# Two float32 blocks on one core: the slots of the split-weight ring get different offsets within 64 bytes

## What is computed

```python
def squared_relu_mlp(hn, w_up, w_down):
    return jnp.square(jax.nn.relu(hn @ w_up)) @ w_down

def first_block(x, ...):
    h = x
    for i in range(DEPTH):                       # 2
        hn = rmsnorm(h, mix_norm_g[i])
        mix = gated_deltanet(...) if i % N_MIXERS == 0 else moba_layer(...)
        h = h + mix.astype(h.dtype)
        h = h + squared_relu_mlp(rmsnorm(h, mlp_norm_g[i]), mlp_w_up[i], mlp_w_down[i])
    return rmsnorm(h, final_norm_g)
```

## Time and profile before

| | |
|---|---|
| median of 3 runs | 1252.89 us (1252.87 to 1253.22) |
| span of the profiled execution, first to last instruction | 1249.1 us |
| the profiled execution's own time | not recorded apart; the median is 3.8 us over the span |
| instructions in the span | 21,521 |
| moved by DMA | 210.80 MB |

### The profile page before, as it was taken

One profiled execution on the slowest core, in us unless ns is written; L12 is line 12 of the kernel. 1 busy time (PEld: TensorE's weight loads), 2 busy tenths in 40 slices (PEclk: granted clock), 3 DMA queues, 4 the chain that ended last, 5 costly groups with the idle time before them and its releaser, 6 DMA issues.

```text
span 1249.1 us, 21521 instructions
## 1 busy us (share of the span) xinstructions
PE 1220.7 (98%) x8583; PEld 1106.9 (89%) x8583; DVE 871.6 (70%) x1252; ACT 700.5 (56%) x1016; POOL 56.3 (5%) x102
## 2 busy tenths in 40 slices
PE   8999989999999999999999999999999999999997
PEld 7999988888888998888888999999999977888886
DVE  5888567666666656666656589998656577778876
ACT  4984555555455554554554564656454456666663
POOL 5010020000000001000000000000000010000000
PEclk9999999999999999999999999999999999999999
DMA  7671134666554654565555565354546534555561
GB/s 223 197 203 68 38 122 150 222 214 202 186 184 151 203 165 141 166 211 180 184 185 167 172 210 184 118 162 145 179 150 203 186 107 147 174 194 190 201 201 68
DMA packets 160340, 210.80 MB, mean 169 GB/s; under 512 B 5542, under 2 KB 143220, under 8 KB 160261
## 3 DMA queue, kind: packets, MB, share of 16 engines
q1 hardware_dynamic: 157315, 202.77, 50.6%
q0 software_dynamic: 1904, 6.85, 1.4%
q10 hardware_dynamic: 1042, 0.07, 0.1%
HBM read 208.62 MB, written 1.05 MB: 168 GB/s over the span
## 4 chain that ended last, share of the span: by engine, by line
PE 79%; DVE 10%; ACT 4%; issue 2%; DMA 2%; SPq 1%; POOL 1%; DVEq 0%; POOLq 0%; ACTq 0%
PE bank L369 16%; PE bank L373 16%; PE bank L372 16%; PE bank L454 15%; PE bank L450 8%; DVE wlo L305 3%; ACT whi L297 2%; PE bank L1425 2%; DMA raw<-in_dn_w_in 1%; DVE common L2582 1%; PE bank L2003 1%; PE bank L1445 1%; ACT common L753 1%; SPq L3388 1%; PE bank L2095 1%
## 5 line engine op out<-in xcount | busy, mean ns | idle before, releaser
L305 DVE TENSOR_TENSOR wlo<-raw,whi 128x2048 fp32r<-128x2048 f32 x190 | 434.9, 2291 | 203.6 <-ACT whi L297 203.3
L297 ACT ACTIVATE whi<-raw 128x2048 fp32r<-128x2048 f32 x190 | 363.3, 1913 | 145.4 <-PE bank L369 43.5
L369 PE MATMUL bank<-xparts,whi 128*128 128x256 f32 x912 | 262.5, 288 | 0.4 <-DVE common L2764 0.4
L373 PE MATMUL bank<-xparts,wlo 128*128 128x256 f32 x912 | 258.7, 284 | 0.0
L372 PE MATMUL bank<-xparts,whi 128*128 128x256 f32 x912 | 258.6, 284 | 0.0
L454 PE MATMUL bank<-xparts,whi 128*128 128x512 f32 x832 | 208.0, 392 | 0.0
L369 PEld LDWEIGHTS bank<-xparts,whi 128*128 128x128 f32 x912 | 175.5, 192 | 2.8 <-issue 2.1
L372 PEld LDWEIGHTS bank<-xparts,whi 128*128 128x128 f32 x912 | 175.6, 192 | 0.6 <-issue 0.5
L373 PEld LDWEIGHTS bank<-xparts,wlo 128*128 128x128 f32 x912 | 175.5, 192 | 0.0
L454 PEld LDWEIGHTS bank<-xparts,whi 128*128 128x128 f32 x832 | 149.8, 189 | 26.9
L369 PE MATMUL bank<-whi,hhi 128*128 128x512 f32 x392 | 153.1, 391 | 3.8 <-DVE hlo L1061 2.3
(11 more groups left out here) (391 smaller groups left out, 1706.2 us busy)
## 6 DMA issues: line engine op xcount, KB each, us to landing
raw<-in_mlp_w_up SPq DMA_DIRECT2D x32, 1024.0 KB, 5.5
raw<-in_mlp_w_down SPq DMA_DIRECT2D x32, 1024.0 KB, 5.1
raw<-in_w_in SPq DMA_DIRECT2D x22, 1024.0 KB, 5.3
raw<-in_w_up SPq DMA_DIRECT2D x22, 1024.0 KB, 5.2
raw<-in_w_gate SPq DMA_DIRECT2D x16, 1024.0 KB, 5.5
raw<-in_dn_w_in SPq DMA_DIRECT2D x15, 1024.0 KB, 5.8
raw<-in_mb_w_in SPq DMA_DIRECT2D x12, 1024.0 KB, 5.2
raw<-in_w_down SPq DMA_DIRECT2D x11, 1024.0 KB, 4.9
```

What stands on the lines that cost most here:

```text
L297: nc.scalar.activation(whi[:, s, :], raw[:, r, :], ACT.Copy).then_inc(hi_ready, 1)
L305: nc.vector.tensor_tensor(wlo[:, s, :], raw[:, V % RAW, :], f32(whi[:, s, :]), ALU.subtract).then_inc(lo_ready, 1)
L369: ins = pe.matmul(o, shi, mhi, start=first, stop=False, skip_group_check=True)
L373: return pe.matmul(o, slo, mhi, start=False, stop=last, skip_group_check=True)
```

## The change

Each ring becomes one flat tile that is 16 float32 (64 bytes) longer, and `whi` and `wlo` become lists of four views into it. Slot s of `whi` starts 4 s float32 further than before, slot s of `wlo` 4 s + 2 further.

```diff
-        whi = sb("whi", [P, RING, UNIT], F32R)
-        wlo = sb("wlo", [P, RING, UNIT], F32R)
+        whi_ring = sb("whi", [P, RING * UNIT + 16], F32R)
+        wlo_ring = sb("wlo", [P, RING * UNIT + 16], F32R)
+        whi = [whi_ring[:, s_ * UNIT + 4 * s_:(s_ + 1) * UNIT + 4 * s_] for s_ in range(RING)]
+        wlo = [wlo_ring[:, s_ * UNIT + 4 * s_ + 2:(s_ + 1) * UNIT + 4 * s_ + 2] for s_ in range(RING)]
...
-            nc.scalar.activation(whi[:, s, :], raw[:, r, :], ACT.Copy).then_inc(hi_ready, 1)
+            nc.scalar.activation(whi[s], raw[:, r, :], ACT.Copy).then_inc(hi_ready, 1)
...
-            nc.vector.tensor_tensor(wlo[:, s, :], raw[:, V % RAW, :], f32(whi[:, s, :]),
+            nc.vector.tensor_tensor(wlo[s], raw[:, V % RAW, :], f32(whi[s]),
                                     ALU.subtract).then_inc(lo_ready, 1)
...
         def wview(w, s, k):
-            return w[:, s, :].rearrange("p (k n) -> p k n", k=k)
+            return w[s].rearrange("p (k n) -> p k n", k=k)
```

More of the change, by code:

```diff
@@ L319, in first_split_hi @@
             act.wait_ge(raw_in[0] if half else first_in, 16)
-            nc.scalar.activation(whi[:, 0, FIRST[half]], raw[:, 0, FIRST[half]], ACT.Copy)\
+            nc.scalar.activation(whi[0][:, FIRST[half]], raw[:, 0, FIRST[half]], ACT.Copy)\
                 .then_inc(hi_ready if half else first_hi.sem, 1)
@@ L328, in first_split_lo @@
                 dve.wait_ge(first_hi.sem, first_hi.value)
-            nc.vector.tensor_tensor(wlo[:, 0, FIRST[half]], raw[:, 0, FIRST[half]], f32(whi[:, 0, FIRST[half]]),
+            nc.vector.tensor_tensor(wlo[0][:, FIRST[half]], raw[:, 0, FIRST[half]], f32(whi[0][:, FIRST[half]]),
                                     ALU.subtract).then_inc(lo_ready if half else first_lo.sem, 1)
```

## The result

The changed kernel takes **1256.53 us** (median of 5 runs, 1255.4 to 1258.86), the kernel before 1252.87 us (5 runs, 1251.13 to 1253.22). The ratio is **1.0039 [1.0028, 1.0049]**: slower by 0.4%, where 1249.2 us and a small gain had been forecast. The profiled execution took 1256.44 us itself, with a span of 1254.7 us, 5.6 us more than the span before.

What follows compares the result with a forecast made beforehand. The prediction took TensorE's time per matmul as the bound; its terms -6.9 - 0.8 + 3.9 + 0 - 0.5 made -4.3 us of steps, times 0.87 -3.7 us, so 1252.9 became 1249.2 us, range 1237 to 1260 us.

Steps and rivals of the forecast that it cites:

- The bound: Whole kernel: TensorE busy 98% of the span and holding 79% of the chain, so its time per matmul matters most.
- ACT, DVE, DMA and waits at nothing: Splits writing the ring at new places, loads and waits: costed at nothing, 0.4 us at most for the splits.
- The signs of the groups: TensorE steps: with xparts moving from 120 to some 118 ns, over hhi and hlo from 226.7 to some 230, differing by slot.
- The premise that carried the sizes: TensorE steps over bhi/blo: a 32-byte shift within 64 goes with 2.2 ns less per short matmul, 6.6 ns more per long.
- Ring moving, 512 columns: 1,176 long steps over hhi and hlo at 226.7 ns: 3.3 ns more each, +3.9 us.
- L454: 832 MLP steps at 230 ns: no change, 0, bounds -2.7 and +5.0 us.
- ring stationary, 256 columns: 3,120 short steps of 120 ns, xparts over the ring or ring over xparts: 2.2 ns less each, -6.9 us.
- L450: 832 short MLP steps at 118.8 ns, taken to 117.8: -0.8 us.
- bhi and blo: Products with these tiles: 480 short steps stay at 117.8 ns, 144 long ones go from 233.3 to 230, -0.5 us.
- The factor 0.87: Share of the counted TensorE steps on the chain, 887 of 1,021 us; it scales -4.3 us of steps to -3.7 us.
- The slower rival: TensorE: long matmuls lose their lock, +9.1 us on the path, short ones gain nothing; 1262.0 us, chance 0.30 for slower.
- The best-lock rival: TensorE: every shape locks at its best, short steps at 114 ns, long at 226.7; 24.5 us less, 1228.4 us, chance 0.08.

Runs made afterwards that it cites:

- b_on_64: Kernel before the change with bhi and blo moved by 32 bytes, to a multiple of 64, rings as before; one time of 1252.82 us against 1252.07.
- tiles_only: Changed kernel with all eight slots back at offset 0, so only the tiles behind the longer rings lie elsewhere; ratio 0.9993, median 1251.25 us.
- x32: Kernel before the change with xparts moved by 32 bytes and all tiles behind it by 64, rings as before; ratio 1.0021, median 1255.07 us.
- slots_only: Changed kernel's slot offsets, but each ring 256 bytes longer than before the change instead of 64; ratio 1.002, median 1254.84 us.
- x_192_again: Second measurement of the kernel before the change with xparts 192 bytes further and all behind it 256 further; ratio 0.994, median 1243.32 us.
- feat_at_0: Changed kernel with only gemm_rows units keeping the offsets, all others at 0, slots 64 bytes further apart; ratio 1.0002, median 1252.66 us.
- x_192: Kernel before the change with xparts 192 bytes further and all behind it 256 further; ratio 0.9952, median 1246.35 us.
- x_64: Kernel before the change with xparts 64 bytes further and all behind it 256 further; ratio 0.9945, median 1246.33 us.
- x_192_lo256: Kernel before the change with xhi 192 and xlo 256 bytes further, all behind them 256 further; ratio 0.9989, 1250.26 us.
- rows_at_0: Changed kernel with gemm_rows units (512 ring columns moving) at offset 0, others keeping the offsets, slots 64 bytes further apart; ratio 1.0006, median 1252.1 us.

## Why the prediction was wrong

The time lies in the forecast range and has the wrong sign. Step by step:

- **The bound: right.** TensorE's steps set the time; everything found is in them.
- **ACT, DVE, DMA and waits at nothing: right.** L307 and L299 have 2291 and 1915 ns against 2291 and 1913, and no wait joined the chain.
- **The signs of the groups: mostly right.** Steps with xparts got shorter, the ones over hhi and hlo longer, and both differ by slot.
- **The premise that carried the sizes: wrong.** "With 256 columns and bhi or blo moving, 32 bytes past a multiple" and its long counterpart were read as what 32 bytes do. b_on_64 took those 32 bytes away and the long steps kept 233.3 ns; tiles_only and x32 changed hhi's steps by 4 to 6 ns without moving ring, hhi or hlo off multiples of 64. What the runs support instead is the distance between the two operands over some 256 bytes, and the change altered that by 64 to 128 bytes as well, in a part of the diff that I had cost at nothing since "their place within 64 bytes stays".
- **The term "Ring moving, 512 columns": too small.** +3.3 ns was taken, +5.6 measured, in every slot: means of 231.7, 233.3, 233.5 and 231.5 in slots 0 to 3. The forecast had slot 0 spared because its high weights stay; but hhi moved by 128 bytes against it, and slots_only has 232.5 in slot 0 even without that, with wlo 8 bytes further. That is 6.5 us in place of 3.9.
- **L454: 0 taken, +2.5 ns measured**, 2.1 us, within its bounds.
- **The term "ring stationary, 256 columns": a third of its size.** -2.2 ns was taken, -0.7 measured for xparts over the ring and -0.6 for the ring over xparts, -2.3 us in place of -6.9. This is the largest error: 4.6 us. The row that it was sized by, bhi over the ring, lies at a distance of 32 bytes, where x32 has 116.9 for xparts as well; the change made distances of 8 to 128 bytes, and its stretches of short steps have means from 118 to 122. L450 came out as forecast (-0.7, taken -0.8).
- **bhi and blo: the short ones got 1.3 ns longer**, +0.6 us, where no change was taken.
- **The factor 0.87: near enough for this change.** 6.2 us of steps became 5.6 us of span, 0.90, since the loss lies in the MLPs, which TensorE bounds. It is not right for gains elsewhere: x_192_again realised half of 17.1 us, and in x32 gains and losses of steps nearly cancel (+0.8 us in all) while the median rose by 3.0.

The misses sum to 4.6 + 2.6 + 2.1 + 0.6 and some 0.5 us of the small groups, 10.4 us of steps; -4.3 + 10.4 = 6.1, which is the +6.2 measured. The slower rival (all long ones lose their lock, the short ones gain nothing, 1262.0 us) had the mechanism; the short steps' small gain and 5.6 in place of 6.6 ns make up the rest. The best-lock rival (1228.4 us) asked that all short steps go to 114 with the long ones at 226.7: x_192_again comes near it with 114.4 and 227.6, but half of its gain became waits for other engines and loads, which that rival left out.

By the Trainium skill, page "SBUF — State Buffer", section "SBUF: two separate sides", TensorE never waits on anyone at its side of SBUF, and the prediction worked out from it that nothing would change. Here the steps over hhi go from 226.9 ns to 233.2 in x32 by a move of 64 bytes, with equal shapes and equal work on the other engines. Whether the longer step is a wait on anyone, or arises inside TensorE, no run here shows.

**Left open.** Why slot offsets and the move of the tiles cost more together than apart. No run moved both operands by the same bytes, which would test the distance against the places directly; for it speaks the agreement of feat_at_0 with x_192 and x_64. P took 256 for the period and missed several of its times and steps, as told above. A move of xparts alone by 256 bytes, which P says does nothing, was not tried; that 256 counts as 0 rests on the long steps over hhi. What inside TensorE makes the distance count is only argued: a reading of moving columns and next weights that meet, and lock. And single distances do not tell all: three products take turns in `mm3`, as x_192_lo256 shows; in tiles_only, hhi's steps at distances of 128 (whi) and 192 (wlo) take 231.1 ns, where rows_at_0 has 233.2 and 233.3 at each of them alone; and one kernel has two locks.

## What to carry to other kernels

When TensorE's step is longer than its columns, compare the step of one shape over tiles at different places, to the nanosecond and start to start, and move one tile alone before moving several: here one line that moves `xparts` by 192 bytes, with all else kept at multiples of 256, is worth 0.5 to 0.6%, while spreading the slots cost 0.4%. A row of the trace that differs in offset differs in tile and distance too; take it as evidence on the offset only once something that moves nothing else agrees. Look at the steps stretch by stretch before trusting a mean, and in a second execution: it can hide two levels. And a gain in TensorE's steps counts only where TensorE isn't soon waiting for another engine's work.

## What the runs showed of the hardware

In these runs a float32r matmul's step depends on the distance between its operands' addresses. With d the bytes from the weights to the moving operand, modulo 256, and shapes, order and waits alike (means in ns, one execution each):

| group (kernels) | d = 0 | 32 | 64 | 192 |
|---|---|---|---|---|
| short, xparts over ring (before, x32, x_64, x_192) | 119.9 | 116.9 | 117.3 | 114.7 |
| short, L450 (the same) | 119.1 | 117.1 | 117.4 | 115.5 |
| long, L454 (the same) | 230.0 | 233.2 | 229.8 | 233.2 |

The first row's 117.3 and 114.7 mix locks at 113 to 114 and 118 ns; at d = 0 every stretch is at 120. For the long steps of the ring over hhi, d = 0 has 226.9 (before), and 227.6 and 228.5 where hhi is 256 bytes further (x_192, x_64); d = 192 has 233.2 (x32). In rows_at_0 its slots stand at d = 0, 64, 128 and 192, and have means of 227.3, 229.9, 233.3 and 233.2. So 128 does not act as 0, and 256 nearly does. Short and long shapes want different distances: 192 has the lowest mean seen for the short ones and is among the worst for the long. In the kernel before, both rings, xparts, hhi and hlo happened to lie at d = 0, which is the best for the steps over hhi and the slowest in this table for the short ones. I had not expected that the place of a tile, with no instruction changed, moves a whole program by 0.4% up or 0.6% down; nor that odd starts would cost ACT and DVE nothing to be measured (DVE's split 2289 to 2291 ns and ACT's 1911 to 1915 in every kernel).
